# Two residual norms computed in context and latent halves, values before queries and keys, and a twelve-slot expert ring that gathers its tokens pair by pair

## The reference

```
for i in range(2):                       # first block
    xn, xc = modulate(rmsnorm(h), ..), modulate(rmsnorm(hc), ..)   # shift and scale differ for h and hc
    y, yc = diff_attention(xn, xc)       # i = 0      (neighbourhood_attention in i = 1)
    h  = h  + g_m * y ;  h  = h  + g_f  * swiglu(modulate(rmsnorm(h), ..))
    hc = hc + cg_m * yc; hc = hc + cg_f * swiglu(modulate(rmsnorm(hc), ..))    # i = 0 only
x = rmsnorm(h)
# second block
x = x + (conv branch + latent attention) @ w_mix_out
x = x + memory_cross_attention(rmsnorm(x), rmsnorm(mem))
x = x + expert_choice_moe(rmsnorm(x))    # 16 experts, 32 tokens each, width 1024
return rmsnorm(x)
```

## Time and profile before

| | us |
|---|---|
| median of three runs (2166.5 to 2174.7) | 2170.7 |
| the profiled execution's own time | 2169.1 |
| its span, first to last instruction | 2167.3 |
| TensorE matmuls busy | 1928.1 (89%) |
| DVE busy | 768.7 (35%) |
| ScalarE busy | 299.6 (14%) |

### The profile page before, as it was taken

The page is one execution under the profiler, slowest core; times in us unless marked ns, Lnnn a source line. Parts: engine busy times, 40 slices in busy tenths (PEclk is TensorE's granted clock), DMA queues, the critical chain, the costliest instruction groups (busy, mean ns, idle before and its releaser), DMA issues.

```text
span 2167.3 us, 22077 instructions
## 1 busy us (share of the span) xinstructions
PE 1928.1 (89%) x8678; PEld 1277.4 (59%) x8678; DVE 768.7 (35%) x1425; ACT 299.6 (14%) x703; POOL 85.5 (4%) x123
## 2 busy tenths in 40 slices
PE   8999999899999998998999999999998876556665
PEld 5585463588886445844788888886887411111111
DVE  6697684576853413207321102125122300000001
ACT  2200370210110001006200000014001200000000
POOL 1011000000000123000000000000000000000000
PEclk9999999999999999999999999999999988888787
DMA  9465202254443573311354534441472799999996
GB/s 356 156 223 167 106 1 78 68 179 152 159 159 108 185 162 92 98 58 39 98 154 148 180 129 137 154 143 54 155 261 108 298 414 422 422 421 423 421 422 290
DMA packets 86014, 422.64 MB, mean 195 GB/s; under 512 B 9840, under 2 KB 9968, under 8 KB 60912
## 3 DMA queue, kind: packets, MB, share of 16 engines
q1 hardware_dynamic: 70416, 364.10, 45.2%
q0 software_dynamic: 15520, 57.45, 7.9%
HBM read 420.47 MB, written 2.95 MB: 195 GB/s over the span
## 4 chain that ended last, share of the span: by engine, by line
PE 75%; DMA 17%; DVE 5%; issue 1%; ACT 1%; SPq 0%; DVEq 0%; ACTq 0%
PE ps L650 35%; PE ps L672 8%; DMA hT<-in_up 6%; PE ps L790 5%; DMA hT<-in_down 5%; DMA hT<-in_gate 4%; PE ps L1129 4%; PE ps L692 3%; PE ps L702 3%; PE ps L728 3%; PE ps L848 3%; PE ps L719 2%; PE ps L881 2%; PE ps L905 2%; DVE small L1762 1%
## 5 line engine op out<-in xcount | busy, mean ns | idle before, releaser
L650 PE MATMUL ps<-big,ring 128*128 128x256 f32 (+1 forms) x1088 | 313.9, 450 | 11.4 <-DMA ring<-in_memkv 9.9
L650 PE MATMUL ps<-xn,ring 128*128 128x256 f32 (+1 forms) x1376 | 310.3, 386 | 5.2 <-ACT xn L1241 3.7
L650 PEld LDWEIGHTS ps<-xn,ring 128*128 128x128 f32 x1376 | 261.1, 191 | 53.9 <-issue 13.5
L650 PEld LDWEIGHTS ps<-big,ring 128*128 128x128 f32 x1088 | 207.4, 191 | 115.5 <-issue 84.0
L1129 PE MATMUL ps<-ring,aux 128*32 128x512 f32 x768 | 156.7, 737 | 83.1 <-DMA ring<-in_up 31.1
L2006 DVE TENSOR_TENSOR work<-work,ps 128x512 f32<-128x512 f32 x8 | 8.3, 1040 | 419.1 <-PE ps L1129 419.1
L650 PE MATMUL ps<-aux,ring 128*128 128x257 f32 x704 | 153.4, 380 | 0.0
L650 PEld LDWEIGHTS ps<-aux,ring 128*128 128x128 f32 x704 | 133.6, 190 | 19.1 <-issue 0.4
L1129 PEld LDWEIGHTS ps<-ring,aux 128*32 128x32 f32 x768 | 32.5, 120 | 169.9 <-issue 169.9
L1602 DVE SCALAR_TENSOR_TENSOR aux<-aux,scond 128x1024 f32<-128x1024 f32 x94 | 115.2, 1277 | 4.3 <-DMA aux<-in_ada 4.3
L790 PE MATMUL ps<-ring,xn 128*128 128x512 f32 x256 | 111.5, 593 | 2.1 <-issue 2.1
(11 more groups left out here) (276 smaller groups left out, 2238.1 us busy)
## 6 DMA issues: line engine op xcount, KB each, us to landing
ring<-in_gate SPq DMA_DIRECT2D x48, 1024.0 KB, 14.9
ring<-in_up SPq DMA_DIRECT2D x48, 1024.0 KB, 15.3
ring<-in_gu SPq DMA_DIRECT2D x88, 512.0 KB, 3.5
ring<-in_down SPq DMA_DIRECT2D x42, 1024.0 KB, 15.6
aux<-in_ada POOLq DMA_DIRECT2D x80, 512.0 KB, 4.9
ring<-in_wqkv SPq DMA_DIRECT2D x48, 512.0 KB, 4.1
ring<-in_down SPq DMA_DIRECT2D x32, 704.0 KB, 4.1
ring<-in_win SPq DMA_DIRECT2D x44, 512.0 KB, 3.4
```

Source lines behind the costliest of these rows:

```text
L650: mm = pe.matmul(ps[:, bank(s, c), 0:T], ring[:, slot(s.u0, j), k * P:(k + 1) * P], rhs(kk), start=kk == 0, stop=kk == nk - 1)
```

## The change

Five edits.

**1. `n1` in halves.** `wo0` becomes `wo0` (four chunks, 512 tokens) and `wo0h` (four chunks, first all context halves, then all latent halves; `halved`). TensorE's parts of the context norm `n1c` stand between the latent halves of the rows; `n1l`, the latent norm, stands inside the first products of the feed-forward. The feed-forward's first pair is computed without the seven-product scheme (`plain`): gate and up for context, and after `n1l` for latent. The scheme starts at pair 1, and the modulation work is one pair later. SyncE reloads a slot of `wo0h` only after the latent half has used it.

**2. `n2` in halves.** `down0` gives its last two chunks to `down0h`, halved in the same way, with `n2c` inside; `n2l` stands in the first two tiles of the stage that follows.

**3. Values first.** That stage is now `v1`, whose tiles 0 and 1 take context tokens and 2 and 3 latent ones. Then come `q1` and `k1`. `k1`'s sums of tokens move to the columns of the weight ring that units of 512 KB leave free.

**4. Mask.** The bias mask is added by DVE, in eight parts, before `k1`'s sums of weights, and not by GpSimd.

**5. Experts.** Twelve slots: the four new ones lie in `aux`, `work` and the two parts of `xn`. Before the products only the first pair's tokens are gathered; every pair gathers the next one's tokens after its turn (`gathered`). The scatter matrices are made for each pair by DVE from a row of token numbers (one matmul in `memo`) and two columns of choices. The last pair stands outside the loop.

The diff, cut:

```diff
-EXPERT_SLOTS = 8
+EXPERT_SLOTS = 12
-        Stage("wo0", ("wo0", 0), 8, 8, "D"),
-        Stage("gu0", ("gu0", 0), 2 * FC, 2 * FC, "AD"), Stage("down0", ("down0", 0), 16, 8, "D", WIDE),
+        Stage("wo0", ("wo0", 0), 4, 4, "D"), Stage("wo0h", ("wo0", 4), 4, 8, "D", halves=4),
+        Stage("gu0", ("gu0", 0), 2 * FC, 2 * FC, "AD", plain=1), Stage("down0", ("down0", 0), 12, 6, "D", WIDE),
+        Stage("down0h", ("down0", 12), 4, 4, "D", WIDE, halves=2), Stage("v1", ("wqkv1", 16), 8, 8, "A", share=(4, 4)),
         Stage("q1", ("wqkv1", 0), 8, 8, "A"), Stage("k1", ("wqkv1", 8), 8, 8, "AD"),
-        Stage("v1", ("wqkv1", 16), 8, 8, "A", share=(4, 4)),
...
+        expert_ring = [halves[:, 0].rearrange("p k t -> p (k t)"), aux[:, 3072:5120]] + expert_ring\
+            + [work[:, 0:DOUBLE], xn_flat[:, 0:DOUBLE], xn_flat[:, DOUBLE:2 * DOUBLE],
+               halves[:, 1].rearrange("p k t -> p (k t)")]
...
                         elif n == 1:
+                            sp.wait_ge(s_osb, JOBS["mla"][3])
+                        elif n == 2:
                             sp.wait_ge(s_used, u0)
+                        elif n == 8:
+                            sp.wait_ge(s_part, NORM["nmoe"]["n"] + 1)
+                        elif n == 9:
+                            sp.wait_ge(s_moe, 2)
                         elif n == EXPERT_SLOTS - 1:
                             sp.wait_ge(s_seed, 1)
...
+                if s.plain:
+                    early, late = slice(0, CTX), lat
+                    plain(0, 0, early, NORM["n1c"]["a0"])
+                    norm_sums("n1l")
+                    plain(1, 1, early, middle=lambda: norm_stat("n1l"))
+                    first(1)
+                    norm_bc("n1l")
+                    second(1)
+                    plain(0, 0, late, NORM["n1l"]["a0"])
+                    plain(1, 1, late).then_inc(s_used, 2)
...
-            norm_whole("n1")
+            halved(st["wo0h"], lambda k, later: xn[:, k, lat if later else slice(0, CTX)], KC,
+                   {(4, 0): lambda: norm_sums("n1c"), (5, 0): lambda: norm_stat("n1c"), (6, 0): lambda: norm_bc("n1c")})
...
-            norm_whole("n2")
-            rows(st["q1"], lambda k: xn[:, k, lat], LAT, ready=(s_nA, NORM["n2"]["a0"] + 1))
+            halved(st["down0h"], lambda k, later: hid[:, k, lat if later else slice(0, CTX)], FC,
+                   {(2, 0): lambda: norm_sums("n2c"), (2, 1): lambda: norm_stat("n2c"), (3, 0): lambda: norm_bc("n2c")})
+            def value_steps():
+                steps = {(0, k): lambda k=k: pe.wait_ge(s_nA, NORM["n2c"]["a0"] + k + 1) for k in range(KC)}
+                steps[1, 0] = lambda: norm_sums("n2l")
+                steps[1, 3] = lambda: norm_stat("n2l")
+                steps[2, 0] = lambda: pe.wait_ge(s_nA, NORM["n2l"]["a0"] + 8)
+                return steps
+            tokens(st["v1"], lambda k, q: xn[:, k, q * P:(q + 1) * P], 4, lambda c: norm_bc("n2l") if c == 1 else None,
+                   value_steps())
+            rows(st["q1"], lambda k: xn[:, k, lat], LAT)
             seven(st["k1"], lead=False)
-            tokens(st["v1"], lambda k, q: xn[:, k, q * P:(q + 1) * P], 4)
...
+            def gathered(choices):
+                for k in range(KC):
+                    for q in range(2):
+                        mm = pe.matmul(ps[:, 6, k * 2 * CAP:(k + 1) * 2 * CAP], hs[:, q, k * P:(k + 1) * P], choices[:, q, :],
+                                       start=q == 0, stop=q == 1)
+                return mm
...
                 pe.wait_ge(s_hT, i + (pair + 1))
+                if not last:
+                    pe.wait_ge(s_psel, i + (pair + 1))
+                    gathered(pair_sel).then_inc(s_gath, 1)
...
-            with pe.Fori(0, NE // 2 - 1) as i:
+            with pe.Fori(0, NE // 2 - 2) as i:
                 pair_steps(i, 1, 16)
+            pair_steps(NE // 2 - 2, 1, 16, last=True)
```

More of the change, by code:

```diff
@@ L119, in plan @@
         s.m0 = pairs
[L120 removed]
+        pairs += s.chunks // 2 - s.plain if s.owner == "AD" else 0
         a += {"A": s.chunks, "D": 0, "AD": s.chunks // 2}[s.owner]
@@ L730, in last, with plain @@
                     mm.then_inc(s_used, 2)
-                if lead:
+                def plain(at, unit, tokens, ready=None, middle=None):
+                    landed(s.u0, 0, unit)
+                    for k in range(KC):
+                        if ready:
+                            pe.wait_ge(s_nA, ready + k + 1)
+                        if middle and k == 4:
+                            middle()
+                        mm = pe.matmul(ps[:, at, tokens], ring[:, slot(s.u0, unit), k * P:(k + 1) * P],
+                                       xn[:, k, tokens], start=k == 0, stop=k == KC - 1)
+                    return mm
[9 more added lines that the diff above has]
+                    plain(1, 1, late).then_inc(s_used, 2)
+                elif lead:
                     first(0)
@@ L736, in seven @@
                     second(1)
-                for m in range(s.chunks // 2):
+                for m in range(s.plain, s.chunks // 2):
                     if m >= 2 or not lead:
@@ L866, in first_heads, with halved @@
                     part(c, range(4, KC)).then_inc(s_used, 1)
-                for c in range(4, s.chunks):
-                    landed(s.u0, 0, c)
-                    bank_free(s, 0, c)
-                    part(c, range(KC)).then_inc(s_used, 1)
+            def halved(s, rhs, nk, between):
+                n = s.halves
+                parts = s.units // n
+                for j in range(2 * n):
+                    c = j % n
+                    bank_free(s, 0, j)
+                    for part in range(parts):
+                        landed(s.u0, 0, c * parts + part)
+                        for k in range(nk // parts):
+                            kk = part * (nk // parts) + k
+                            mm = pe.matmul(ps[:, bank(s, j), 0:LAT], ring[:, slot(s.u0, c * parts + part), k * P:(k + 1) * P],
+                                           rhs(kk, j // n), start=kk == 0, stop=kk == nk - 1)
+                        if j >= n:
+                            mm.then_inc(s_used, 1)
+                        elif part == parts - 1:
+                            mm.then_inc(s_chunk, 1)
+                        if (j, part) in between:
+                            between[j, part]()
             def attention(name):
@@ L1042, in _, with token_numbers @@
             heads_read("mem")
-            rows(st["memo"], lambda k: x2[:, k, :], LAT)
+            def token_numbers(c):
+                if c == 2:
+                    pe.wait_ge(s_tokd, 1)
+                    pe.matmul(ps[:, 7, 0:LAT], ones, gx[:, 0, :], start=True, stop=True).then_inc(s_tokr, 1)
+            rows(st["memo"], lambda k: x2[:, k, :], LAT, between=token_numbers)
             norm_whole("nmoe")
@@ L1111, in product @@
-            def product(i, base, part, lhs, ahead=False, between=None):
+            def product(i, base, part, lhs, ahead=False):
                 for kk in range(4):
@@ L1185, in square_inputs @@
         def square_inputs(name, k):
-            added = {"n1": "wo0", "n2": "down0", "n3": "wo1", "nfm": "down1", "nq2": "mix", "nmoe": "memo"}
+            for norm, whole in (("n1", "wo0"), ("n2", "down0")):
+                if name[:2] == norm:
+                    s, h = st[whole], st[whole + "h"]
+                    if k < s.chunks:
+                        return s_freeD, s.d0 + k + 1
+                    return s_freeD, h.d0 + (h.halves if NORM[name]["later"] else 0) + k - s.chunks + 1
+            added = {"n3": "wo1", "nfm": "down1", "nq2": "mix", "nmoe": "memo"}
             if name in added:
```

356 lines of the change are left out of this document (205 added, 151 removed).

## The result

The changed kernel takes 2140.5 us in the median (2137.7 to 2141.2, four runs), the kernel before beside it 2168.6 (2166.2 to 2174.7): a ratio of 0.986, 95% interval 0.984 to 0.989. The forecast was 2142. A second set of runs gave 2143.1 against 2170.4, ratio 0.9875 (0.986 to 0.989). The profiled execution took 2141.2 us with a span of 2139.4, which is 27.9 us less than before.

The account below looks back on a forecast made before the run. TensorE bounds the kernel to about 1700 us, then the DMA stream at 422 GB/s. Experts 16.5, n1 7.8 and n2 4.2 sum to 28.5 us off 2169.1: 2140.6, median forecast 2142, main range 2134 to 2148, 8 in 10 2133 to 2156.

Parts of the forecast that it names:

- norm n1: From `wo0`'s last row to the first regular feed-forward pair: 40.9 us become 32.8, less 0.3, gain 7.8 (4 to 10).
- n2: Second norm with values first and mask: 147.5 us become 143.3, gain 4.2 us (bounds 1 to 8).
- the first release: Experts: the first slot is released to the stream at 1702.4, 3.0 us earlier, as only the first pair's tokens are gathered.
- the ramp: Start of the experts' stream: 5.9 us lost before; with twelve slots covering the first pair, gain 4.0 us.
- the prediction's own sign: Prediction is wrong if gaps stand at each half's norm, TensorE ends the loop's waits, or an edit misses by over 3 us.
- Two regimes: To about 1700 us TensorE is the chain, a gap worth its whole length; then DMA's stream, counting start and bytes left.
- The stall before `v1`'s tile 2: Tile 2 waits for all eight shifts of `n2l`: 3.8 us, plus 1.5 us for the lower clock.
- the gather "at nothing": Next pair's gather in each expert pair, 3.84 us on TensorE: costed at nothing, since TensorE was busy 59% of a pair.
- the mask: 9.8 us on DVE, some 50 us ahead of its readers, costs nothing; GpSimd's 17.5 us go, off the chain.
- Rival 1: Experts' slots are filled but the end doesn't follow: 9.9 + 4.0 us lost, 2156; chance 0.12.
- Rival 2: The norms' overlaps fail, each half's chain is late and the clock falls: 7.8 + 4.2 shrink to 2, 2152; chance 0.10.
- Rival 3: TensorE becomes the experts' bound: 65.8 us a pair against 59.6 of stream, +43 us, 2185; chance 0.04.

Follow-up runs that it names:

- two gathers: The changed kernel with every gather in the pair loop issued twice, same result: 2148.2 us, ratio 0.9901 against the kernel before.
- the norms alone: The changed kernel without its edit to the experts (eight slots, all tokens gathered before the first pair): 2157.5 us, ratio 0.994 against the kernel before.
- four gathers: The changed kernel with every gather in the pair loop issued four times: 2214.8 us, ratio 1.0199 against the kernel before.

## Why the prediction was right, step by step

**Right in kind, and in size partly by cancelling.** The span fell by 27.9 us where 28.5 were said, but the terms were off by more than their sum: norm n1 +1.3 (and 0.25 from before it), n2 +0.2, the first release -0.2, the ramp -3.7, and a chance +1.6 at the end. By the prediction's own sign, a single edit that gives over 3 us other than said, it missed twice: edit 4 was worth 7 to 9 us and not nothing, and edit 5, without the chance at the end, 12.6 and not 16.5. What held is the frame. Two regimes, and a price for each: every gap taken from TensorE's chain before 1700 us came through whole, and the experts' stream followed the DMA queue. The first release came 16.1 us sooner (13.3 carried over, 2.8 of its own, predicted 3.0), 8.0 us behind the seeding where 7.7 were said. The stall before `v1`'s tile 2 was read off the code at 3.8 us and is 4.00; its clock was put at 1.5 and cost about 3. That `n2` gained 4.4 all the same, by the terms below, makes the 4.2 partly luck.

**Too dear: the norm's parts.** The prediction took 1.65 + 0.61 + 0.70 = 2.96 us for each half from `nmoe`, where each part follows a wait. Among products without a gap, they delay the next one by 1.00 (399.90 - 398.90), 0.37 (402.10 - 401.73) and about 0.5: 1.9 each. Four of them (two in each stage) are 4.3 us: 2.1 of the surplus belongs to `n1`, which is more than the 1.3 by which it beat its forecast, and 2.1 to `n2`, where it paid for the clock.

**Wrong: the ramp.** The step "5.9 us lost ... gain 4.0" brought 0.3 (10.2 for four slots and ramp together, of which the slots are 9.9). The last landing is 434.6 us behind the first release, not 431. It stands 7.2 us behind first release + 172 x 2.485 in the changed kernel, and 7.5 behind 176 x 2.485 before. Most of it is no loss that slots could repair: 1.6 us pass from the issue to the first data, 1.2 are the final weights, and 2 to 3 are left that I put down to the landing itself (what remains when all else is subtracted; not measured alone). Only a shortfall is a ramp, and a window of the changed kernel shows how much there is:

```profile
1700.00:1750.00 50.00, 38.64 (x260) 15.59 (x256) 4.49 (x11) 2.23 (x4) 0.56 (x1) 0.86 1.00 409
```

It is 50 x (1 - 409/422) = 1.5 us. Counted from the first data to the last slower window, it is 2.4 us before (406 GB/s from 1706.96 to 1770) and 2.2 after (407 from 1690.9 to 1750, 419 to 1760): there never were 4 us to gain. I had compared a landing with a sum of transfer times and taken the constant between them for idle time.

**Right for a poor reason: the gather "at nothing".** In the loop that holds, with 11.6 us to spare. In the first pair the same cover doesn't exist: there, only the four slots bought by the same edit hide it, as the runs with eight slots and with two gathers show.

**Missed: the mask.** The prediction puts DVE's mask at "nothing" and has GpSimd's go "off the chain". DVE's did cost nothing. But with `n2c` moved under `down0h` GpSimd's mask would have met it, and edit 4 is what saves the other edits 7 to 9 us. Even before, it was not quite off the chain: `norm_bc` of `n2` waits 3.68 us there, that of `n1`, with no mask beside it, 3.02. The row stands in the trace of the kernel before: an instruction on two to four elements that takes 0.83 us where its neighbours take 0.16, and ends at 840.21, when the mask of the earlier trace rows ends (822.69 + 17.49 = 840.18). From the timeline of DVE in the kernel before:

```profile
839.19 0.16 DVE L1526 TENSOR_SCALAR small<-ps 128x4 f32<-128x4 f32 x1 [3.61 <-PE ps L822]
839.38 0.83 DVE L1489 TENSOR_SCALAR small<-small 128x4 int32<-128x4 int32 x1
840.25 0.16 DVE L1491 TENSOR_TENSOR small<-small 128x4 f32<-128x4 f32 x1
```

TensorE's wait behind it:

```profile
842.76 2.08 PE L839 MATMUL ps<-work,cst 128*128 128x512 f32 x2 [3.68 <-DVE work L1537]
```

**Not predicted: the tail.** Its 1.6 us are the last 16 records, 1.98 us at full clock where they took 3.62. Other traces of kernels with the changed tail show 1.98 to 3.66 for these records, so it is chance and not the change.

**The rivals.** Rival 1 (the end doesn't follow) didn't come: 422 GB/s were kept, and a pause worth 11.1 us was seen only with eight slots. Rival 2 fell with the norms alone. Rival 3 was 17.8 us too high for a pair: it took all products at 1.2 GHz.

## What to carry to other kernels

Price a slot of a prefetch ring by the longest stretch in which its reader frees nothing, and look for that stretch in the first round, where no backlog exists; the steady loop will not show it. When two engines' work is brought side by side for the first time, read the length of the smallest instructions there: one of a few elements that takes microseconds is held by the other engine, though nothing in the profile calls it a wait (9.97 us for 0.17 here). And where a wait of a few microseconds stands between dense products, price the clock behind it too: here 4.00 us of waiting cost about 3 more.

## What the runs showed of the hardware

- Loads of 1 MB with eleven in flight instead of seven: 422 GB/s in both, and 26 to 27 us instead of 17.3 from issue to landing.
- A busy TensorE is not a fast one. In the run with four gathers, 128 records of 64 columns follow each other without a gap for 27 us, and the granted clock stays at half:

```profile
1712.35:1739.30 26.95, 26.95 (x128) 26.84 (x128) 0.00 (x0) 0.00 (x0) 0.00 (x0) 0.51 0.90 374
```

- A wait of 4.00 us ahead of dense products was followed by nearly 6 us at half clock; waits of 0.97 and 1.20 us by none.
